# The feature norm's logarithm and exponential ahead of a tile's copies on ScalarE, and the mixer's first tile loaded within the delta net

## The reference, cut to what matters

```python
def l2_normalize(x):
    return x * lax.rsqrt(jnp.sum(x * x, axis=-1, keepdims=True) + EPS)

def gdn_mixer(qkv, a, b, gate, conv_w, conv_prev, A_log, dt_bias, norm_g, S0):
    ...
    y, conv_new = causal_dwconv(qkv, conv_w, conv_prev)
    y = jax.nn.silu(y.astype(f32))
    nkd = GDN_HEADS * GDN_DK
    q = l2_normalize(y[..., :nkd].reshape(B, T, GDN_HEADS, GDN_DK)) * (GDN_DK ** -0.5)
    k = l2_normalize(y[..., nkd:2 * nkd].reshape(B, T, GDN_HEADS, GDN_DK))
    ...
    S, o = lax.scan(_gdn_chunk, S0.astype(f32), tuple(to_chunks(z, c) for z in (q, k, v, g, beta)))
    ...

def ssd_mixer(z, xbc, dt, conv_w, conv_b, conv_prev, A_log, dt_bias, D_skip, norm_g, h0):
    ...
    h, ys = lax.scan(_ssd_chunk, h0.astype(f32), tuple(to_chunks(u, c) for u in (xs, dts, a, Bm, Cm)))
    ...
```

## Time and profile before

| | us |
|---|---|
| median of 3 runs | 4369.09 (4368.46 to 4374.56) |
| the profiled execution | 4367.9 |
| its span | 4365.8 |

### The profile page before, as it was taken

How to read it: one execution, slowest core, us unless ns; L and a number is a source line. 1 busy time by engine, 2 the same in 40 slices (tenths; PEclk the granted TensorE clock), 3 DMA queues, 4 the chain that set the end, 5 groups by cost and what they waited for, 6 DMA issues and landing times.

```text
span 4365.8 us, 49384 instructions
## 1 busy us (share of the span) xinstructions
PE 4051.1 (93%) x20340; PEld 2189.5 (50%) x20340; DVE 1397.9 (32%) x2792; ACT 979.6 (22%) x1659; POOL 260.9 (6%) x384
## 2 busy tenths in 40 slices
PE   6788898889999999999999979978899999999998
PEld 3454456645455555555545435565454555554554
DVE  2236674662311111100022456647513212121001
ACT  2026662431100000000011366434301000000000
POOL 0000031400000000000000000414000000000000
PEclk9899998899999999999999989978999999999999
DMA  5410133142122122111122101423311111111111
GB/s 200 114 60 29 36 96 99 59 175 102 60 97 87 59 68 68 59 51 42 57 74 76 59 25 56 123 74 113 117 41 41 34 34 34 34 34 32 36 36 52
DMA packets 186849, 299.48 MB, mean 69 GB/s; under 512 B 89056, under 2 KB 140448, under 8 KB 180224
## 3 DMA queue, kind: packets, MB, share of 16 engines
q1 hardware_dynamic: 182144, 279.35, 19.5%
q0 software_dynamic: 3904, 12.27, 0.9%
q10 hardware_dynamic: 576, 4.72, 0.3%
HBM read 245.30 MB, written 42.47 MB: 66 GB/s over the span
## 4 chain that ended last, share of the span: by engine, by line
PE 87%; DVE 4%; ACT 2%; issue 2%; POOL 1%; DMA 1%; DVEq 1%; ACTq 1%; SPq 1%; POOLq 0%
PE PS L804 51%; PE PS L1380 16%; PE PS L1351 6%; PE PS L832 2%; PE PS L782 1%; PE PS L1227 1%; DVE big L1768 1%; PE PS L927 1%; DVE xT L1771 1%; PE PS L1281 1%; PE PS L1305 1%; POOL xT L2423 1%; DVE hT L1771 1%; PE PS L1264 1%; PE PS L1246 1%
## 5 line engine op out<-in xcount | busy, mean ns | idle before, releaser
L804 PE MATMUL PS<-hT,ring 128*128 128x512 f32 (+1 forms) x6816 | 2243.7, 491 | 34.6 <-ACT hT L1449 21.2
L804 PEld LDWEIGHTS PS<-hT,ring 128*128 128x128 f32 x6816 | 1135.3, 192 | 1152.1 <-issue 1138.0
L1380 PE MATMUL PS<-big,ring 128*128 128x512 f32 (+1 forms) x2112 | 683.5, 487 | 2.5 <-DVE big L1771 2.5
L1380 PEld LDWEIGHTS PS<-big,ring 128*128 128x128 f32 x2112 | 346.6, 191 | 339.4 <-issue 336.5
L1768 DVE SCALAR_TENSOR_TENSOR xT<-PS,mod,xT 128x1024 f32<-128x1024 f32 x32 | 41.1, 1284 | 856.9 <-PE PS L1380 642.0
L1437 ACT ACTIVATE hT<-xT 128x1152 f32<-128x1152 f32 x40 | 46.3, 1162 | 929.0 <-DVEq L2288 804.2
L1351 PE MATMUL PS<-big,ring 128*128 128x512 f32 (+1 forms) x768 | 250.3, 487 | 1.0 <-DVEq L2227 1.0
L2316 DVE TENSOR_SCALAR big<-fext,par 128x1024 f32<-128x1024 f32 x44 | 35.7, 812 | 671.2 <-ACTq L1736 671.2
L1560 ACT ACTIVATE xT<-big,tk 128x1024 bf16<-128x1024 f32 x186 | 223.5, 1202 | 52.0 <-DVEq L1908 47.2
L1734 ACT ACTIVATE fext<-PS 128x1024 f32<-128x1024 f32 x44 | 45.1, 1025 | 839.8 <-PE PS L804 839.8
L1880 DVE TENSOR_SCALAR_CACHE_REDUCE xT<-big,tk 128x384 bf16<-128x384 f32 (+6 forms) x268 | 222.8, 832 | 28.0 <-issue 0.9
(11 more groups left out here) (384 smaller groups left out, 3253.4 us busy)
## 6 DMA issues: line engine op xcount, KB each, us to landing
ring<-in_w_ada SPq DMA_DIRECT2D x96, 512.0 KB, 4.9
ring<-in_w_in SPq DMA_DIRECT2D x54, 512.0 KB, 5.2
ring<-in_w_gate SPq DMA_DIRECT2D x44, 512.0 KB, 3.5
ring<-in_w_up SPq DMA_DIRECT2D x44, 512.0 KB, 3.5
ring<-in_w_down SPq DMA_DIRECT2D x32, 448.0 KB, 3.3
d_x<-big SPq DMA_DIRECT2D x24, 576.0 KB, 4.6
ring<-in_kidx SPq DMA_DIRECT2D x16, 512.0 KB, 4.8
ring<-in_w_out SPq DMA_DIRECT2D x16, 512.0 KB, 5.6
```

What stands on the lines that cost most here:

```text
L804: i = mm(pset(n % 2)[:, c0:c0 + m], w[:, k, :], hT[:, k, c0:c0 + m], start=(k == 0), stop=(k == KT - 1))
L1380: i = mm(pset(m % 2)[:, c0:c0 + n], w[:, k - k0, :], act[:, k * TOK + c0:k * TOK + c0 + n], start=(k == 0), stop=(k == NF - 1))
```

## The change

It does two things. In ScalarE's program `l2_scale(n - LEAD - 3)` stands ahead of `conv_rows(n)`, where it stood behind it. In SP's program `load_s(0)` stands behind the gate loads and ahead of the wait for the delta net's output; tiles 1 and 2 follow that wait as before. For that the slots are renumbered, so that tile 0 goes to `xw[:, 7432:8968]` (it went to `hw[:, 4840:6376]`) and tile 2 to the latter; tile 1 keeps its place.

```diff
--- before.py
+++ after.py
@@ -467,7 +467,7 @@
 
             return ap.rearrange("p h (c t) -> p h c t", t=64)
 
-        sl = [z.rearrange("p (c k x) -> p c k x", c=2, k=12) for z in (xw[:, 7432:8968], hw[:, 4840:6376], big[:, 2 * TOK:2 * TOK + 1536])]
+        sl = [z.rearrange("p (c k x) -> p c k x", c=2, k=12) for z in (xw[:, 7432:8968], big[:, 2 * TOK:2 * TOK + 1536], hw[:, 4840:6376])]
 
         def two_tiles(x, c, k):
 
@@ -487,7 +487,7 @@
         hs_scaled = [big[:, o_qk + 1024 * q:o_qk + 1024 * q + 1024] for q in range(3)] + [fext[:, 0:1024]]
         def tile_in(t):
 
-            return sl[(t + 1) % 3], sl_in[(t + 1) % 3], t // 3 + 1
+            return sl[t % 3], sl_in[t % 3], t // 3 + 1
 
         hb = [xw[:, 4096 + 512 * i:4608 + 512 * i] for i in range(3)]
         h_end = xw[:, 5632:6144]
@@ -680,8 +680,9 @@
                 sp.wait_ge(*g_wtc.at(l, 5))
                 for hp in range(2):
                     sp.dma_start(gt[:, hp, :], a["scr"][14 + hp]).then_inc(*gt_in.up())
+                load_s(0)
                 sp.wait_ge(*g_out.at(l, 3))
-                for t in range(3):
+                for t in range(1, 3):
                     load_s(t)
                 sp.dma_start(hs, a["sstate"][l]).then_inc(*state_in.up())
                 for t in range(3, NT):
@@ -1563,9 +1564,9 @@
 
                 silu_tile(NROT)
                 for n in range(LEAD, LEAD + NCONV):
-                    conv_rows(n)
                     if 0 <= n - LEAD - 3 < 5:
                         l2_scale(n - LEAD - 3)
+                    conv_rows(n)
                     if n > LEAD:
                         conv_silu(n - 1)
                         if n - LEAD - 1 < 5:
```

## The result

The changed kernel takes 4307.4 us (median of 4 runs, 4303.1 to 4309.0) beside 4368.8 for the kernel before on the same chip: a ratio of 0.9857, 95% interval 0.9842 to 0.9873. That is 61.4 us less, where 63.8 was forecast, and the time lies 2 us above the 4305.3 predicted. The profiled execution took 4305.9 us (span 4303.8).

The account below looks back on a forecast made before the run. TensorE, busy 93% of the span, was taken as the bound: ending its waits for ScalarE's exponential gives 62.4 us and the earlier mixer load 1.4, together 63.8, so 4305.3 us; 8 in 10 for 4299 to 4325.

Parts of the forecast that it names:

- it doesn't do what it says: Rival: TensorE's sums really wait for the squares, so the logarithm's place changes nothing; only 1.4 us won, 4367.7; chance 0.04.
- slower: Rival: the logarithm delays the copies by up to 4.83 us, 5 tiles x 2 layers, 48 us; 4417; chance 0.03.
- The new bound: Tiles 11 to 14: ScalarE's turn of 19.2 to 20.1 us exceeds the 17.40 TensorE needs, so it bounds four turns.
- 28.7 us: Layer 0: gain up to the start of TensorE's sums after tile 14, before anything the clock gives.
- 2.5 were taken for the clock: Last sums and tile 15: full clock on TensorE gives 2.5 us more a layer, bounds 0 to 2.5.
- Predicted 16 us in both layers: Sign of being right: TensorE's idle time before the feature norm's sums falls from 60.1 to about 16 us.
- low clock: Rival: TensorE's remaining waits end at 1.2 GHz, 5.0 us less gain; 4310.3; chance 0.09.
- ScalarE's turn grows: Rival: holds like the 3.26 us one in three turns a layer add 19.6 us; 4324.9; chance 0.10.
- VectorE is held: Rival near tile 16: VectorE held for all of GpSimd's 8.86 us, 7.2 us less gain; 4312.5; chance 0.08.
- more than 1 us: Sign of being wrong: ScalarE waits for VectorE before its second count for more than 1 us.
- Taking 0: Tile 16 on: TensorE's wait for VectorE's first difference taken as 0, range 0 to 2 us.
- Part 2: First mixer tile loaded earlier, ending waits of 0.78 and 0.65 us; 1.4 us won, bounds 0 and 1.5.

Follow-up runs that it names:

- e1: Kernel before with only the logarithm and exponential moved ahead of the copies on ScalarE; 4308.6 us, ratio 0.9856.
- e7: Kernel before with the logarithm and exponential ahead of the copies only in the turns of tiles 11 and 12; 4344.0 us, ratio 0.994.
- e4: Changed kernel with two extra copies on ScalarE at the head of its turns for tiles 11 to 14; 4319.7 us, ratio 0.989.
- e5: Kernel before with two extra copies on ScalarE at the head of its turns for tiles 11 to 14; 4368.6 us, ratio 0.9995.
- e8: Changed kernel with each of GpSimd's large subtractions cut into four; 4311.9 us (one run).
- e9: Changed kernel with GpSimd's four subtractions done twice over; 4313.8 us (one run).
- e10: Changed kernel run once more, on one further chip; 4302.3 us, ratio 0.9843 of the kernel before.
- e2: Changed kernel with ScalarE's old order, so only the first mixer tile is loaded sooner; 4370.6 us, ratio 1.0001.

## Why the prediction was right, point by point

**The cause.** The waits stood for the exponential, and the exponential stood behind copies that needed a tile. e1 gives the whole gain of the stretch with the order alone, e7 27.9 of its 63.0 us with two of the four waits. The rival "it doesn't do what it says" is out, and so is "slower", which would have shown at the copies of tiles 12 to 15.

**The new bound.** The prediction said that ScalarE's turn of 19.2 to 20.1 us takes over. By the copies in the fence of ScalarE, the turns of tiles 11, 12 and 13 are 384.80 to 404.74, 19.94; 19.59; and 18.98 (predicted 20.08, 19.77 and 19.15). Each was taken 0.14 to 0.18 too long. Most of it is in the 4.83 us for logarithm and exponential, read where a table load follows the exponential; here the copies follow, and they begin 0.09 us before the exponential's row has ended (383.83 + 1.06 against 384.80), so the same steps take 4.72 or 4.73 us. e4 against e5 shows the bound itself.

**The size.** From the sums after tile 10 to those after tile 14 the prediction won 28.7 us, and the rows give 360.90 to 467.38, 106.48, less 366.37 to 443.54, 77.17: 29.3. From there to the decay rows it is 34.34 before and 32.07 after, 2.3 us, where 2.5 were taken for the clock. Together 31.58, predicted 31.2; layer 1 has 31.44. The two small errors have opposite signs.

**The waits that are left.** Predicted 16 us in both layers, measured 11.3. Of the 2.3 us that are missing in a layer, 1.8 lie behind tile 12. The sums after it and tile 13 took TensorE 19.17 us, where the prediction has 17.40, because the clock was granted at 0.61 in the sums and at 0.91 over the whole, and a wait shrinks by what the matmuls ahead of it take longer: 0.42 us are left of some 2.4. The rest is ScalarE's turns, each a little shorter than predicted. The windows of the changed kernel (stretch, length, busy us of PE, PEld, DVE, ACT and POOL, granted clock, DMA share, GB/s):

```profile
404.98:408.06 3.08, 3.08 (x5) 1.34 (x6) 0.89 (x1) 3.00 (x4) 0.00 (x0) 0.61 0.04 16
404.98:424.15 19.17, 19.17 (x52) 9.26 (x52) 14.04 (x33) 17.59 (x22) 0.00 (x0) 0.91 0.01 3
```

This also corrects the rival *low clock*, priced at 5.0 us for its two last sums. Those ran at the full clock (1.10 us for two). Where the clock did fall, after tile 12, it cost the kernel nothing: in the traces of the changed kernel, e1, e8, e9 and e10, two layers each, TensorE still waited 0.42 us for ScalarE behind tile 13, and the stretch was 109.21 to 109.24 each time. The four sums alone took between 2.41 and 3.60 us there, but with tile 13 it was 19.17 or 19.18 every time, so these runs don't show what a longer stretch at the lower clock would cost. While ScalarE is the bound, a slower TensorE only waits less, here by 1.8 us with 0.4 left.

**ScalarE's turn grows; VectorE is held.** The first did not happen; ScalarE waits for VectorE before its second count 1.38, 1.02, 1.03 and 1.37 us in the four turns, where it was 1.38, 1.02, 1.02 and 1.03 before. The prediction's sign for it, "more than 1 us", was set badly: the waits were above it already. For the second the prediction took a hold of 3.3 us and kept 8.86 as the rival. It read GpSimd's row x4 as one thing. It is four instructions, and e8 and e9 show that the unit of the hold is one of them. The Trainium skill (SBUF — State Buffer, SBUF: two separate sides) states this: the port pair that VectorE and GpSimd share is locked by one instruction for its whole length, against VectorE instructions in a two-port mode, or with two SBUF inputs where GpSimd reads SBUF. By it one hold is at most 3.6 us, and the rows agree; that several can follow one another, e9 shows. The sentence on contention from which the prediction priced the rival says which instructions contend and gives no length, so it did not speak for a hold of 8.86 us.

**Tile 15 and 16.** The copies of tile 16 follow those of tile 15 after 17.06 us (461.24 to 478.30), taken as 17.4 within 16.5 to 21.3, and no wait stands at line 936. Taking 0 there was right.

**Part 2.** 1.4 us were taken, and 1.9 show in the rows, because an idle time starts at the end of a pipelined row (e2). The load was hidden as said: it went out right behind the gate loads, and these landed after 4.1 us, at some 699, no later than without it (4.3 us in the kernel before); VectorE first reads them at 724.72. SP's issues in layer 0 of the changed kernel, and two lines of the DMA table of that stretch (KB each, median us to landing):

```profile
693.72 0.82 SPq L682 DMA_DIRECT2D big<-scr  x2
694.58 0.43 SPq L678 DMA_DIRECT2D xT<-d_x  x1
```
```profile
big<-scr SPq DMA_DIRECT2D x2, 576.0 KB, 4.1
xT<-d_x SPq DMA_DIRECT2D x1, 768.0 KB, 7.0
```

## What to carry to other kernels

When the bound engine waits for a result, look at what stands in the producing engine's queue ahead of it, and at whether that engine is idle with the input ready: then the order costs time and the work doesn't. After a reorder the new bound is the length of the other engine's turn, so price it before; a few us of added work in the old and in the new order tell which of the two bounds holds. Work that was free in the idle time, here a second table load and a search round, becomes worth removing once the turn is the bound.

## What the runs showed of the hardware that was not expected

**A wait's length alone doesn't say whether the clock falls.** In e4, TensorE was granted 1.00 through a wait of 3.3 us and in the sums behind it, and 1.00 through one of 4.5 us but 0.54, near the 1.2 GHz level, in the sums behind that:

```profile
383.05:386.30 3.25, 0.00 (x0) 0.00 (x0) 1.04 (x4) 3.19 (x4) 0.00 (x0) 1.00 0.46 161
386.35:388.30 1.95, 1.95 (x5) 0.99 (x6) 0.00 (x0) 1.95 (x3) 0.00 (x0) 1.00 0.00 0
403.80:408.30 4.50, 0.02 (x1) 0.02 (x1) 2.09 (x6) 4.42 (x5) 0.00 (x0) 1.00 0.36 117
408.30:412.00 3.70, 3.69 (x5) 1.64 (x6) 1.50 (x2) 3.60 (x5) 0.00 (x0) 0.54 0.00 0
```

In layer 1 of e4 the wait before the first of these sums was 3.30 us as in layer 0, and the sums behind it ran at 0.59:

```profile
2510.42:2513.64 3.22, 3.22 (x5) 1.44 (x6) 1.03 (x1) 3.13 (x4) 0.00 (x0) 0.59 0.00 0
```

In the changed kernel a wait of 2.47 us, shorter than these, was followed by 0.61, and a wait of 3.5 us after tile 14 of e4 by sums at the full clock. What decides it the runs don't show.

**Which VectorE instructions GpSimd holds.** Tiny products, bit operations and selections on 128 x 7 were held, one with a single input among them (3.50 us against 0.17), and so were the convolution's taps on 128 x 1024 (4.73 and 4.61 us against 1.29), while count passes over 128 x 384 to 128 x 768 beside the same GpSimd work kept their 0.6 to 1.0 us. It goes the other way as well: beside these taps in e9 GpSimd's instructions of 64 x 256 took 1.41 us, where they take 0.61.

**A switch of ScalarE's table cost its own row and no more on this path.** The logarithm starts 1.30 us after the start of its table load (399.08 to 400.38), and leaving out a load of 1.28 us shortened the way by 1.27.
